# Low parts of the input weight tiles on GpSimd, and the third conv tile's taps all on VectorE

## The reference

```python
h = modulate(rms_norm(x, norm1_g), sh1, sc1)        # shift and scale from silu(c) @ w_ada
z = h @ w_in                                        # 1024 -> 1536: a, gate, u (512 each)
hc = a * jax.nn.sigmoid(gate)
hc, new_buf = causal_depthwise_conv(hc, conv_buf, conv_w, conv_b)   # width 31, 512 channels
hc = jax.nn.silu(layer_norm(hc, conv_ln_g, conv_ln_b))
hs, hT_re, hT_im = s5_mixer(u, ...)                 # 32 groups, complex diagonal scan, then GLU
x = x + g1 * (concatenate([hc, hs]) @ w_out)
h2 = modulate(rms_norm(x, norm2_g), sh2, sc2)
x = x + g2 * peer_ffn(h2, ...)                      # product-key retrieval over 16384 experts
y = modulate(rms_norm(x, final_norm_g), shift, scale)
```

## Time and profile before

| | |
|---|---|
| time, median of 3 runs | 1756.22 us (1754.37 to 1756.67) |
| the profiled execution | 1754.0 us, span 1752.2 us |
| PE busy | 1701.8 us, 97% of the span |
| DVE busy | 1126.4 us, 64% |
| ACT busy | 669.8 us, 38% |
| POOL busy | 805.4 us, 46% |
| chain that ended last | PE 90%, DVE 4%, ACT 2%, POOL 2% |

### The profile page before, as it was taken

How to read it: one execution, slowest core, us unless ns; L and a number is a source line. 1 busy time by engine, 2 the same in 40 slices (tenths; PEclk the granted TensorE clock), 3 DMA queues, 4 the chain that set the end, 5 groups by cost and what they waited for, 6 DMA issues and landing times.

```text
span 1752.2 us, 34387 instructions
## 1 busy us (share of the span) xinstructions
PE 1701.8 (97%) x13743; PEld 1561.7 (89%) x13743; DVE 1126.4 (64%) x3010; ACT 669.8 (38%) x1220; POOL 805.4 (46%) x683
## 2 busy tenths in 40 slices
PE   5999999999999999999999999999999999999996
PEld 2985697999999999999999999998888888888886
DVE  8989833299993766666666660166666666666654
ACT  2323433333333444444444443443333333333334
POOL 1200031345554333333333444467777777777730
PEclk8999999999999999999999999999999999999998
DMA  8554634488988787888987888689999999999971
GB/s 307 143 159 171 138 125 164 145 227 244 242 238 244 218 253 235 242 260 251 261 242 226 258 260 253 211 327 342 390 389 378 362 374 347 380 384 368 372 279 62
DMA packets 307711, 458.54 MB, mean 262 GB/s; under 512 B 27008, under 2 KB 217648, under 8 KB 305504
## 3 DMA queue, kind: packets, MB, share of 16 engines
q1 hardware_dynamic: 273648, 355.86, 64.1%
q0 software_dynamic: 33904, 100.48, 16.0%
HBM read 396.27 MB, written 127.10 MB: 299 GB/s over the span
## 4 chain that ended last, share of the span: by engine, by line
PE 90%; DVE 4%; ACT 2%; POOL 2%; DMA 1%; issue 1%; ACTq 0%; DVEq 0%; POOLq 0%
PE ps L2017 42%; PE ps L2051 25%; PE ps L1710 8%; PE ps L1996 5%; PE ps L2006 4%; POOL gathered_act L656 1%; PE ps L1642 1%; PE ps L1909 1%; DMA v_rows_ring<-v_rows,v_row_index 1%; PE ps L1964 1%; PE ps L1800 1%; POOL v_rows_ring L665 0%; PE ps L1851 0%; PE ps L1880 0%; DMA act_spill<-actr 0%
## 5 line engine op out<-in xcount | busy, mean ns | idle before, releaser
L2017 PE MATMUL ps<-h,hl 128*128 128x256 f32 (+1 forms) x6144 | 812.9, 287 | 0.0
L2017 PEld LDWEIGHTS ps<-h,hl 128*128 128x128 f32 x6144 | 758.6, 189 | 0.1
L877 ACT ACTIVATE hl<-raw 128x512 fp32r<-128x512 f32 x512 | 322.2, 630 | 683.5 <-PE ps L2017 468.6
L648 POOL TENSOR_TENSOR hl<-raw,hl 128x512 fp32r<-128x512 f32 x260 | 357.2, 1376 | 470.9 <-ACT hl L877 470.6
L2051 PEld LDWEIGHTS ps<-WH,hl 128*128 128x128 f32 x3072 | 472.3, 188 | 40.3 <-issue 38.6
L2051 PE MATMUL ps<-WH,hl 128*128 128x336 f32 x3072 | 486.8, 318 | 1.3 <-ACT actr L910 1.3
L1574 DVE TENSOR_TENSOR hl<-raw,hl 128x512 fp32r<-128x512 f32 x252 | 176.0, 699 | 206.1 <-ACT hl L877 205.0
L656 POOL DMA_INDIRECT gathered_act<-act_spill,act_index x184 | 213.8, 1162 | 62.4 <-issue 55.0
L1503 DVE TENSOR_SCALAR ohA<-ps,selT 128x128 f32<-128x128 f32 x336 | 117.2, 349 | 163.3 <-PE ps L2006 151.5
L665 POOL DMA_INDIRECT v_rows_ring<-v_rows,v_row_index x184 | 181.5, 987 | 82.5 <-issue 50.1
L1504 DVE TENSOR_SCALAR ohB<-ps,selT 128x128 f32<-128x128 f32 x336 | 134.9, 402 | 0.0
(11 more groups left out here) (305 smaller groups left out, 1266.3 us busy)
## 6 DMA issues: line engine op xcount, KB each, us to landing
raw<-in_u SPq DMA_DIRECT2D x128, 512.0 KB, 6.3
v_rows<-in_v SPq DMA_DIRECT2D x128, 512.0 KB, 5.8
raw<-in_v SPq DMA_DIRECT2D x128, 512.0 KB, 7.5
act_spill<-actr SPq DMA_DIRECT2D x128, 260.0 KB, 3.1
raw<-in_w_ada SPq DMA_DIRECT2D x64, 512.0 KB, 4.4
gate_spill<-stage SPq DMA_DIRECT2D x21, 1024.0 KB, 7.3
hring<-act_spill SPq DMA_DIRECT2D x128, 168.0 KB, 6.0
gbp<-gate_spill SPq DMA_DIRECT2D x16, 1344.0 KB, 8.4
```

Of the source, the lines that this page charges most:

```text
L648: pool.tensor_tensor(hl[:, n % 2, 1, c], raw[:, n % NRAW, c], hl[:, n % 2, 0, c].bitcast(F32), ALU.subtract).then_inc(s_wlo, 1)
L877: act.activation(hl[:, n % 2, 0, c], raw[:, n % NRAW, c], ACT.Copy).then_inc(s_whi, 1)
L2017: last = pe.matmul(ps[:, 2 * (m % 2) + h, 0:b - a], hl[:, m % 2, w, q * P:(q + 1) * P], h2[:, r, q, a:b], start=q == 0 and (w, r) == (0, 0 ...
```

## The change

POOL makes all 12 low parts of the input weight tiles, between its DMAs: the stores of u follow in the same places between them, and the ten loads back, which stood together, are put behind the low parts 7, 8 and 9 (`LOAD_AFTER`). DVE's twelve `split_lo` calls are gone. DVE takes 13, 13 and 12 taps in the input projection stage in place of 10, 10 and 10. The third conv tile (tile 2) has all its 31 taps on DVE: the 16 taps of PE, their tap matrices (line 1300), ACT's four copies, PE's joining matmuls and DVE's joining addition are gone.

```diff
@@ -69,8 +69,6 @@
 PRE = 120
 AFTER_SCAN = 37
 CP = CT - 1
-CH = 2
-PT = 16
 CQ = 32
 VR0 = 4
 VG = 2
@@ -215,8 +213,6 @@
         tapd = uflat[:, 0:CW * CQ].rearrange("p (w j) -> p w j", j=CQ)
         idq = uflat[:, CW * CQ:(CW + 1) * CQ]
         csum = h1[:, CT:KD, 0:TP]
-        tapd2 = wt[:, :, :].rearrange("p t c -> p (t c)")[:, 0:PT * CQ].rearrange("p (w j) -> p w j", j=CQ)
-        csum2 = mixin[:, 0:4, 0:TP]
         MQ = (2 * L - 1) * SQ
         Kt = h1[:, 0:2, :].rearrange("p k t -> p (k t)")[:, 0:ST // 4 * MQ].rearrange("p (n m) -> p n m", m=MQ)
 
@@ -419,7 +415,6 @@
             wide, narrow = STAT_BANKS[norm]
             return ps[:, wide, 0:TP], tstat[:, P:P + TS]
 
-        HALF_BANKS = (3, 4, 5, 7)
 
         SELC = 3
 
@@ -463,6 +458,8 @@
         def acc_bank(s):
 
             return 6 - 2 * s
+
+        LOAD_AFTER = {7: (0, 1, 2, 3), 8: (4, 5, 6), 9: (7, 8, 9)}
 
         block = base.enter_context(nc.Block())
 
@@ -607,6 +604,9 @@
                                    ALU.subtract).then_inc(s_lo, 1)
 
             def load_chunk_rows(i):
+                if i == 0:
+                    pool.wait_ge(s_ush, 16 * 2 * CT)
+                    pool.wait_ge(s_const, 1)
                 if i < L:
                     dst, src = U[i * SQ:(i + 1) * SQ, :, 0:NC], ud[:, :, i, :]
                 elif i == L:
@@ -615,14 +615,17 @@
                     dst, src = U[P - SQ:P, :, NC + TS:NC + 2 * TS], usd
                 pool.dma_start(dst, src.rearrange("g q c -> q g c")).then_inc(s_ul, 16)
 
+            split_lo(FSP["in"], hlm)
+            split_lo(FSP["in"] + 1, hlm)
             for t in range(CT):
+                split_lo(FSP["in"] + t + 2, hlm)
                 pool.wait_ge(s_uev, t + 1)
                 pool.dma_start(ud.rearrange("(t g) q i c -> t (g q) (i c)", t=CT)[t], uT[:, t, 0:TP]).then_inc(s_ush, 16)
                 pool.dma_start(usd.rearrange("(t g) q s -> t (g q) s", t=CT)[t], uT[:, t, TP:T]).then_inc(s_ush, 16)
-            pool.wait_ge(s_ush, 16 * 2 * CT)
-            pool.wait_ge(s_const, 1)
-            for i in range(L + 2):
-                load_chunk_rows(i)
+            for w in range(CT + 2, 3 * CT):
+                split_lo(FSP["in"] + w, hlm)
+                for i in LOAD_AFTER.get(w, ()):
+                    load_chunk_rows(i)
 
             pool.wait_ge(s_cpj, 1)
             for w in range(CT):
@@ -815,9 +818,6 @@
                 if t:
                     gelu_y(t - 1)
             gelu_y(CT - 1)
-            act.wait_ge(s_cp, 2)
-            for i in range(4):
-                act.activation(csum2[:, i, :], ps[:, HALF_BANKS[i], :], ACT.Copy).then_inc(s_cpe, 1)
 
             def glu_sigmoid(t):
 
@@ -1155,13 +1155,7 @@
                 dve.scalar_tensor_tensor(h1lo[:, q, 0:TP], h1[:, q, 0:TP], mods[:, SH1 + q, 0:1],
                                          rhi[:, q, 0:TP].bitcast(F32), ALU.add, ALU.subtract).then_inc(s_h1l, 1)
 
-            def first_splits(q):
-                if q == 0:
-                    split_lo(FSP["in"])
-                if q == 7:
-                    split_lo(FSP["in"] + 1)
-
-            apply_norm("rms1", h1, SH1, first_splits)
+            apply_norm("rms1", h1, SH1)
             dve.wait_ge(s_h1s, 1)
             dve.tensor_tensor(h1lo[:, :, TP:T], h1[:, :, TP:T], rhi[:, :, TP:T].bitcast(F32), ALU.subtract)\
                 .then_inc(s_h1l, 1)
@@ -1169,15 +1163,12 @@
                 h1_low(q)
 
             dve.tensor_tensor(XI[:, :, 0:L, :], pw[0], bb[1], ALU.mult)
-            split_lo(FSP["in"] + 2)
             tt(xt, pw[1], bb[0], ALU.mult)
             dve.tensor_tensor(XI[:, :, 0:L, :], XI[:, :, 0:L, :], xt, ALU.add).then_inc(s_Xr, 1)
-            split_lo(FSP["in"] + 3)
             dve.wait_ge(s_Xr, 3)
             for c in range(4):
                 ts = slice(4 * c, 4 * c + 4)
                 cmul([FO[:, 0, ts], FO[:, 1, ts]], powers(PW, 1, ts), over(cm, ts), xt[:, ts])
-                split_lo(FSP["in"] + 4 + c)
             dve.tensor_scalar(FO[:, 1], FO[:, 1], -1.0, None, ALU.mult).then_inc(s_Fr, 1)
             link(dve.memset(hc[:, :, 0:CW - 1], 0.0))
 
@@ -1194,7 +1185,7 @@
 
             taps = [0] * CT
             tapped_at = [0] * CT
-            OWN_TAPS = [0 if u == CP else CW - PT if u == CH else CW for u in range(CT)]
+            OWN_TAPS = [0 if u == CP else CW for u in range(CT)]
             latest = [CP]
 
             def conv_taps(count, tiles):
@@ -1221,22 +1212,16 @@
 
             dve.wait_ge(s_late, 16 * NLATE)
             conv_rows(0)
-            conv_taps(4, (0,))
-            split_lo(FSP["in"] + 8)
-            conv_taps(6, (0,))
-            split_lo(FSP["in"] + 9)
+            conv_taps(13, (0,))
             conv_rows(1)
-            conv_taps(4, (0, 1))
-            split_lo(FSP["in"] + 10)
-            conv_taps(6, (0, 1))
-            split_lo(FSP["in"] + 11)
+            conv_taps(13, (0, 1))
             dve.wait_ge(s_ush, 16 * 2 * CT)
             link(dve.tensor_reduce(idq, ident[:].rearrange("p (b j) -> p j b", j=CQ), AX.X, ALU.add))
             dve.tensor_tensor(tapd, cw[:, CP, :].rearrange("p (w o) -> p w o", o=1).broadcast_to([P, CW, CQ]),
                               idq.rearrange("p (o j) -> p o j", o=1).broadcast_to([P, CW, CQ]),
                               ALU.mult).then_inc(s_tapd, 1)
             conv_rows(2)
-            conv_taps(10, (0, 1))
+            conv_taps(12, (0, 1))
             conv_rows(3)
             for i in range(5):
                 q = (k(20 + 2 * i), k(21 + 2 * i))
@@ -1297,9 +1282,6 @@
                                   ALU.subtract).then_inc(s_rl, 1)
 
             modulations(1)
-            dve.tensor_tensor(tapd2, cw[:, CH, CW - PT:CW].rearrange("p (w o) -> p w o", o=1).broadcast_to([P, PT, CQ]),
-                              idq.rearrange("p (o j) -> p o j", o=1).broadcast_to([P, PT, CQ]),
-                              ALU.mult).then_inc(s_tapd, 1)
 
             def s5_rows(t):
 
@@ -1310,10 +1292,6 @@
             for t in range(2):
                 s5_rows(t)
                 conv_taps(5 if t == 0 else CT * CW, tuple(range(CT)))
-            dve.wait_ge(s_cpj, 2)
-            dve.wait_ge(s_cv, tapped_at[CH])
-            dve.tensor_tensor(cv[:, CH, 0:TP], ps[:, 7, :], cv[:, CH, 0:TP], ALU.add).then_inc(s_cv, 1)
-            tiles_tapped[CH] = sum(taps) + 1
             s5_rows(2)
             dve.wait_ge(s_cve, 1)
             dve.wait_ge(s_stat, STAT["mean"])
@@ -1887,21 +1865,10 @@
             modulation_rows(2, 3, 5)
             pe.wait_ge(s_z, CT)
             pe.wait_ge(s_mods, 2)
-            pe.wait_ge(s_tapd, 2)
-            for w in range(PT):
-                i = w % 4
-                for r in range(4):
-                    o = CQ * ((r + i) % 4)
-                    rows = slice(CQ * r, CQ * r + CQ)
-                    last = pe.matmul(ps[o:o + CQ, HALF_BANKS[i], :], tapd2[rows, w, :],
-                                     hc[rows, CH, CW - PT + w:CW - PT + w + TP], start=w < 4, stop=w + 4 >= PT)
-            last.then_inc(s_cp, 1)
             pe.wait_ge(s_gw, 16 * CT)
 
             def glu(w):
 
-                if w == 1:
-                    pe.wait_ge(s_cpe, 8)
                 if w >= 2:
                     pe.wait_ge(s_gsig, w - 1)
                 for q in range(CT):
@@ -1910,7 +1877,7 @@
                                          start=q == 0, stop=q == CT - 1)
                 last.then_inc(s_glu, 1)
 
-            order = (CP, 0, 1, CH)
+            order = (CP, 0, 1, 2)
 
             def conv_sums(first, last_):
                 column_sums(lambda q: cv[:, order[q], :], CT,
@@ -1920,12 +1887,6 @@
             modulation_rows(2, 5, 6)
             glu(1)
             conv_sums(0, 1)
-            for i in range(4):
-                for c in range(4):
-                    g = CQ * ((c + i) % 4)
-                    last = pe.matmul(ps[CQ * c:CQ * c + CQ, 7, :], ident[:, g:g + CQ], csum2[:, i, :],
-                                     start=i == 0, stop=i == 3)
-            last.then_inc(s_cpj, 1)
             modulation_rows(2, 6, 7)
             glu(2)
             conv_sums(1, CT)
```

## The result

| | median of the runs | runs | profiled execution (span) |
|---|---|---|---|
| before | 1755.30 us | 1753.05 to 1756.67 (4) | 1754.0 (1752.2) |
| after | 1768.61 us | 1767.44 to 1768.88 (4) | 1768.33 (1766.5) |

The changed kernel is slower: 1.0074 times the time of before, 95% interval 1.0059 to 1.0089. That is +13.3 us where +7.0 was forecast, and just outside the range, which ended at 1768. The direction and the kind of loss were right, its size was not.

What follows compares the result with a forecast made beforehand. PE was taken as the bound (busy 97%), with DVE as full in the change's stage. S5 stage 8.4 late, less 2.4 in the tail, plus 1.0 for the clock: +7.0, 1761.0, plus 2.2 to the median: 1763.2 us (1757.5 to 1768).

Steps and rivals of the forecast that it cites:

- two-input instructions of every kind are blocked: On DVE beside POOL's low parts: products and taps with two SBUF inputs each pay 2.1 us per 1024-element low part.
- `conv_rows` free: On DVE in the input stage: `conv_rows`, with one input in SBUF and one in PSUM, is not blocked by POOL.
- POOL's low part 2 asked for in the middle of a product: Input stage: low part 2 waits some 1.3 us for an XI product; PE's tile 2 starts at 61.3, 2.0 late.
- step (a): Start of the input stage: low part 0 free beside `h` rows, low part 1 blocks DVE once; XI starts 1.2 earlier.
- The tail: After the S5 stage: DVE's 55 remaining taps take 38.0 us, and 2.4 us of the delay is given back.
- taps are blocked: Denies the rival that POOL's low parts block only tensor_tensor and leave DVE's taps free: 1759, chance 0.09.
- no-block case: Rival: DVE and POOL run side by side with no block to speak of: 1755, chance 0.09.
- dearer-block rival: Rival: POOL holds DVE for all of its 2.39 us or more per low part: 1766 to 1769, chance 0.06.
- Step (d): Stretch from `conv_rows(0)` to `conv_rows(1)`: 13.7 us where 10.9 before, low parts costing 2.1 and 0.9; tile 9 6.6 late.
- Step (e): Stretch up to `conv_rows(2)`: 14.4 us where 11.7 before, with blocks of 0.9 and 2.1; tile 11 8.4 late.
- PE's waits for DVE before tiles 7, 9 and 11: Sign in the input stage: PE waits for DVE's `stc_sb` before these tiles, some 2.4, 2 and 2 us.
- The clock: Last sum and fourth GLU block: after PE idles about 5 us, the lower clock costs 0 to 2 us, taken as 1.0.

Runs made afterwards that it cites:

- lows_0_to_7: The changed kernel with low parts 8 to 11 back on DVE between the taps, 0 to 7 still on POOL: 1764.31 us, ratio 1.0055.
- lows_on_pool: The kernel before with all 12 low parts on POOL, the third tile's 16 taps still on PE: 1765.72 us, ratio 1.0067.
- v5: Kernel before with third-tile taps on DVE (10, 10, 18), fourth GLU block, sigmoid and `s5_rows` earlier, identity matmuls in two PE gaps: 1752.99 us, ratio 0.9986.

## Why the prediction failed

**What held.** The choice that two-input instructions of every kind are blocked, at about 2.1 us: 2.08 for FO, 2.03 for XI, 2.02 for a tap. `conv_rows` free (1.20 beside a low part); for the `h` rows it was not put to the test. POOL's low part 2 asked for in the middle of a product, 3.21 us for the wait and itself; PE's tile 2 started at 62.98 where 61.3 was said, later by what step (a) left out. The tail: the taps took 38.3 us (180.0 to 218.3; 38.0 said), the last sum would have ended 12.4 late at full clock where the state was 14.5 late, so 2.1 came back (2.4 said). The rivals are out: taps are blocked (2.78 at 102.25), and the no-block case needs a POOL that reads nothing. The measured time does lie in the range of the dearer-block rival (1766 to 1769), but by luck: its blocks of 2.4 us or more are not there (1.8 to 2.3 measured), and PE never waited for a late low part behind tile 2.

**Step (a), mis-sized by 1.7 us.** "Low part 0 meets `h` rows that read PSUM: free." It met the 128x72 gains at 40.69 and cost 1.8. ACT's high part was there before DVE had the modulations, and the instruction's own size does not matter to what it waits. XI started at 56.24 in place of 54.6, and tile 7 was 6.2 late and not 4.5.

**Step (d), mis-sized by 3.7 us; this is the largest.** I placed low parts by PE's old rhythm, 8 half beside `conv_rows(0)` and 10 behind `conv_rows(1)`, 3.0 us in that stretch. It had three whole blocks (2.34, 2.02 and 1.96 us, 6.3 in all), 17.4 us in place of 13.7. Once DVE is later than PE, PE frees the weight buffer, ACT makes the next high part and POOL starts before DVE gets to its next `conv_rows`; each block makes room for one more. lows_0_to_7 takes them out: 13.3 us and tile 9 3.9 us earlier.

**Step (e), wrong in kind.** I put two blocks into the next stretch, 14.4 us, and let DVE hold tile 11. The stretch had none: low part 10 had come before it, low part 11 came beside `conv_rows(2)`. It took 11.4 us (110.83 to 122.22), and PE reached tile 11 at 127.16 without a wait, 3.7 us after `conv_rows(2)` was over. Of PE's waits for DVE before tiles 7, 9 and 11 (some 2.4, 2 and 2 us said) it had 1.23, 5.60 and none. So the 1.8 us that (e) had put on top of tile 9's lateness were not there, and the clock's 2.5, which I had not counted there, stood in their place: by luck two errors nearly cancelled.

**The clock, mis-sized by 2.4 us.** I counted it once, in the tail, at 1.0. It cost 2.7 there (1.2 in the last sum, 1.5 in the GLU block). It fell behind the wait for tile 9 as well, and that cost 2.5 us between tiles 9 and 11, where I had 1.8 for DVE's further delay. I had read from the earlier trace rows what 3.3 us of idle do, and did not apply it to the gaps of 2 to 6 us that my own steps made. The fall behind the wait for tile 2 was free, since tile 7 waited for DVE anyway.

**The sum.** (a) 1.7, (d) 3.7, tile 11 0.7, the tail's give-back 0.3, its clock 1.7: 8.1 us more than +7.0, and the token sums start 15.1 late (226.3 beside 211.3). The end of the span is 14.3 late in the same pair of executions, the medians 13.3 apart.

**Not settled:** the two levels of lows_on_pool, the shorter hold by a one-input POOL operation, and the clock's fall in v5.

## What to carry to other kernels

Before work is moved to POOL, mark every two-input DVE instruction that can stand beside its reads, and charge each with nearly the whole POOL instruction: here DVE paid some 2.1 us for each of eleven low parts that it could have made itself in 1.13. In these rows it pays for the rest of the POOL instruction at the moment when its own starts, so one that begins beside work with an input in PSUM costs less (0.7 for the twelfth). Place these blocks by the times of the changed schedule and not of the old one, since a delayed engine collects more of them. And where a step of the estimate leaves PE idle as long as here (2.5 to 5.6 us), add the slow matmuls behind it, 2.5 us a time here unless something hid them.
